# The second layer's modulation as sums along rows on VectorE

## The reference, cut to what matters

```python
mod_l = jnp.split((jax.nn.silu(c) @ w_mod[i] + b_mod[i])[:, None, :], N_MOD, axis=-1)
mod_c = jnp.split((jax.nn.silu(c_ctx) @ w_mod[i] + b_mod[i])[None, None, :], N_MOD, axis=-1)
h_l = modulate(rms_norm(x, norm1_g[i]), mod_l[0], mod_l[1])
...
x = x + mod_l[2] * y_l
x = x + mod_l[5] * squared_relu_mlp(modulate(rms_norm(x, norm2_g[i]), mod_l[3], mod_l[4]), w_mlp1[i], w_mlp2[i])
```

## Time and profile before

| | us |
|---|---|
| median of 3 runs | 3865.7 |
| lowest and highest run | 3863.07, 3866.2 |
| the profiled execution, span from first to last instruction | 3859.4 |
| TensorE busy in it | 3717.8 |
| VectorE busy in it | 1794.7 |
| ScalarE busy in it | 1380.8 |

### The profile page before, as it was taken

One profiled execution on the slowest core, in us unless ns is written; L12 is line 12 of the kernel. 1 busy time (PEld: TensorE's weight loads), 2 busy tenths in 40 slices (PEclk: granted clock), 3 DMA queues, 4 the chain that ended last, 5 costly groups with the idle time before them and its releaser, 6 DMA issues.

```text
span 3859.4 us, 65224 instructions
## 1 busy us (share of the span) xinstructions
PE 3717.8 (96%) x27522; PEld 3332.3 (86%) x27522; DVE 1794.7 (47%) x3201; ACT 1380.8 (36%) x2792; POOL 467.9 (12%) x564
## 2 busy tenths in 40 slices
PE   7999899999999999999999999999998999999998
PEld 7877777888888887888888789999997888999998
DVE  4454555233234556544455564443445556444444
ACT  3544443122123444422422352342233235234232
POOL 1122220000002422100111100110012110011001
PEclk9999999999999999999999999999999999999999
DMA  5211122333331211232311112222221111222222
GB/s 186 71 61 61 51 76 71 110 105 109 106 108 61 66 51 63 79 98 94 118 50 41 49 50 91 85 83 88 89 86 40 45 55 50 91 90 84 93 93 72
DMA packets 88129, 306.09 MB, mean 79 GB/s; under 512 B 10000, under 2 KB 13200, under 8 KB 87712
## 3 DMA queue, kind: packets, MB, share of 16 engines
q1 hardware_dynamic: 85184, 293.25, 22.7%
q0 software_dynamic: 2656, 8.68, 0.7%
HBM read 299.79 MB, written 2.10 MB: 78 GB/s over the span
## 4 chain that ended last, share of the span: by engine, by line
PE 90%; DVE 4%; ACT 3%; POOL 1%; issue 1%; DMA 0%; SPq 0%; POOLq 0%; DVEq 0%; ACTq 0%
PE bank L576 65%; PE bank L638 6%; PE bank L1089 2%; PE bank L607 2%; PE bank L875 2%; PE bank L914 1%; PE bank L1075 1%; PE bank L733 1%; PE bank L820 1%; PE bank L942 1%; PE bank L967 1%; PE bank L1214 1%; PE bank L954 1%; PE bank L1185 1%; DVE weight_lo L1870 1%
## 5 line engine op out<-in xcount | busy, mean ns | idle before, releaser
L1870 DVE TENSOR_TENSOR weight_lo<-weight_raw,weight_hi 128x1024 fp32r<-128x1024 f32 (+1 forms) x464 | 557.7, 1204 | 552.3 <-ACT weight_hi L1283 552.2
L1283 ACT ACTIVATE weight_hi<-weight_raw 128x1024 fp32r<-128x1024 f32 (+1 forms) x464 | 476.9, 1031 | 617.4 <-PE bank L576 371.3
L576 PE MATMUL bank<-u_hi,weight_hi 128*128 128x256 f32 (+1 forms) x2112 | 611.6, 290 | 2.5 <-DVE weight_lo L1870 2.3
L576 PE MATMUL bank<-u_lo,weight_hi 128*128 128x256 f32 (+1 forms) x2112 | 599.2, 284 | 0.0
L576 PE MATMUL bank<-u_hi,weight_lo 128*128 128x256 f32 (+1 forms) x2112 | 598.4, 283 | 0.0
L576 PE MATMUL bank<-h_hi,weight_hi 128*128 128x512 f32 (+1 forms) x1328 | 484.9, 365 | 16.0 <-DVE h_lo L2283 9.2
L576 PE MATMUL bank<-h_lo,weight_hi 128*128 128x512 f32 (+1 forms) x1328 | 465.1, 350 | 0.0
L576 PE MATMUL bank<-h_hi,weight_lo 128*128 128x512 f32 (+1 forms) x1328 | 464.9, 350 | 0.0
L576 PEld LDWEIGHTS bank<-u_hi,weight_hi 128*128 128x128 f32 x2112 | 399.7, 189 | 28.7 <-issue 23.0
L576 PEld LDWEIGHTS bank<-u_hi,weight_lo 128*128 128x128 f32 x2112 | 399.5, 189 | 0.0
L576 PEld LDWEIGHTS bank<-u_lo,weight_hi 128*128 128x128 f32 x2112 | 398.5, 189 | 0.1
(11 more groups left out here) (279 smaller groups left out, 7375.4 us busy)
## 6 DMA issues: line engine op xcount, KB each, us to landing
weight_raw<-in_w_mlp SPq DMA_DIRECT2D x128, 512.0 KB, 3.5
weight_raw<-in_w_ff SPq DMA_DIRECT2D x128, 512.0 KB, 3.5
weight_raw<-in_w_in SPq DMA_DIRECT2D x92, 512.0 KB, 3.4
weight_raw<-in_w_mod SPq DMA_DIRECT2D x80, 512.0 KB, 4.4
weight_raw<-in_a_w_qkv SPq DMA_DIRECT2D x24, 512.0 KB, 3.8
weight_raw<-in_b_w_qkv SPq DMA_DIRECT2D x24, 512.0 KB, 3.5
first_weight<-in_w_mod SPq DMA_DIRECT2D x16, 512.0 KB, 15.3
weight_raw<-in_w_ret_o SPq DMA_DIRECT2D x16, 512.0 KB, 3.5
```

The lines of the kernel that those rows point to most:

```text
L576: m = e.matmul(view[:, 0:hi - lo], a[:, k, :], b[:, k0 + k, lo:hi], start=(k == 0 and i == 0), stop=(k == kt - 1 and i == 2))
L1283: e.activation(whi[s % N_SPLIT][:, 0:kt, :], raw[n % N_RAW][:, 0:kt, :], ACT.Copy).then_inc(*tick("act_split", ("hi", n)))
L1870: e.tensor_tensor(wlo[s][:, 0:kt, :], raw[n % N_RAW][:, 0:kt, :], whi[s][:, 0:kt, :].bitcast(F32), ALU.subtract).then_inc(*tick("dve_split ...
```

## The change

The second layer's modulation leaves TensorE. `w_mod1` is laid out on the host as its transpose: tile m holds 128 features on the partitions and the 1024 rows of the matrix along the free axis, again 512 KB. Both condition vectors are laid out on all 128 partitions (`c_rows`, 1 MB), loaded from POOL's queue behind the fence `wo` of the first layer into `vector_rows`, which takes the place of the axial table and the rotation's scratch, and put through Silu by ScalarE in the first turn of the side work. For each tile VectorE then runs two SCALAR_TENSOR_TENSOR instructions, one for each vector: product of tile and vector element by element, with the sum along the row (`accum_out`) as a column of `MOD`. The product itself is thrown away, the first into rows 4 and 5 of the scratch, the second over the tile. The second instruction releases the raw buffer. One addition of all biases follows the last tile. The tiles are spread over 53 turns in place of 56. ScalarE waits for the last sums before it squares for the second layer's norm, since that uses the same scratch.

```diff
+        CROWS = sb("vector_rows", [P, 2, D], F32, o_lcl)
...
+        PRODUCT = SCR[:, 4:6, :].rearrange("p a b -> p (a b)")[:, 0:D]
...
+            def modulation_loads(layer):
+                for m in range(6 * KT):
+                    done_with[weight((f"w_mod{layer}", m), split=False)] = ("modp", layer, m)
+                    yield
...
-            last = diffusion_layer(0, modulation(0, 2 * KT, 6 * KT, True),
-                                   paced(modulation(1, 0, 6 * KT, False), 6 * KT, 56))
+            last = diffusion_layer(0, modulation(0, 2 * KT, 6 * KT, True), paced(modulation_loads(1), 6 * KT, 53))
...
-                    e.wait_ge(*(at("modq", layer, m0 - 2) if m0 else at("modq", layer - 1, 46)))
+                    e.wait_ge(*at("modq", layer, m0 - 2))
...
+            def vector_rows():
+                e.wait_ge(*at("crows"))
+                e.activation(CROWS[:, :, :], CROWS[:, :, :], ACT.Silu).then_inc(*tick("act_mod", ("crowss",)))
+                yield
...
                     if q == 3 and layer == 0:
+                        e.wait_ge(*at("modp", 1, 6 * KT - 1))
                         square(("n1", 1), m, span, x_all(m, N_ALL), "xm", layer, q, m)
...
+            def modulation_rows(layer):
+                e.wait_ge(*at("crowss"))
+                for m in range(6 * KT):
+                    n = number[f"w_mod{layer}", m]
+                    w = raw[n % N_RAW][:, :, :].rearrange("p k c -> p (k c)")
+                    e.wait_ge(*at("raw", n))
+                    e.wait_ge(*at("modp", layer, m - 1))
+                    for s, to in enumerate((PRODUCT, w)):
+                        e.scalar_tensor_tensor(out=to, in0=w, scalar=1.0, in1=CROWS[:, s, :], op0=ALU.mult, op1=ALU.mult,
+                                               accum_out=mod_row(layer, m, s)).then_inc(
+                            *tick("dve_mod", ("modp", layer, m)))
+                    if m + 1 < 6 * KT:
+                        yield
+                e.wait_ge(*at("modp", layer, 6 * KT - 1))
+                both = MOD[layer][:, :].rearrange("p (m s) -> p m s", s=2)
+                e.tensor_tensor(both, both, vec("b_mod", 48 * layer, 48).unsqueeze(2).to_broadcast([P, 48, 2]),
+                                ALU.add).then_inc(*tick("dve_mod", *(("modd", layer, m) for m in range(6 * KT))))
+                yield
...
-            diffusion_layer(0, modulation(0, 2 * KT, 6 * KT, True),
-                            paced(modulation(1, 0, 6 * KT, False), 6 * KT, 56))
+            diffusion_layer(0, modulation(0, 2 * KT, 6 * KT, True), paced(modulation_rows(1), 6 * KT, 53))
...
                 fence("wo", layer)
+                if layer == 0:
+                    e.dma_start(CROWS[:, :, :].rearrange("p s k -> p (s k)"), t["c_rows"]).then_inc(
+                        *tick("dma_crows", ("crows",), by=16))
...
+    both = np.stack([a["c"].reshape(-1), a["c_ctx"].reshape(-1)])
+    out["c_rows"] = np.ascontiguousarray(np.broadcast_to(both.reshape(1, -1), (P, 2 * D)))
...
-        out[f"w_mod{i}"] = tiles_of(a["w_mod"][i])
+        out[f"w_mod{i}"] = np.ascontiguousarray(a["w_mod"][i].T.reshape(-1, P, D)) if i else tiles_of(a["w_mod"][i])
```

More of the change, by code:

```diff
@@ L496, in mod, with mod_row @@
             return MOD[layer][:, j:j + 1]
+        def mod_row(layer, m, s):
+            return MOD[layer][:, 2 * m + s:2 * m + s + 1]
         def source(key):
@@ L1829, in scalar_program @@
             first_norm()
-            diffusion_layer(0, modulation(0, 2 * KT, 6 * KT, True),
-                            paced(modulation(1, 0, 6 * KT, False), 6 * KT, 56))
+            diffusion_layer(0, modulation(0, 2 * KT, 6 * KT, True), vector_rows())
             m0, w = KT - TURN, "b_w_qkv"
```

## The result

The changed kernel takes 3900.5 us (median of 4 runs, 3896.9 to 3905.2) against 3865.2 before (4 runs): the ratio is 1.0091, 95% interval 1.0078 to 1.0105. It is slower, by 35 us where 58 were forecast.

The account below looks back on a forecast made before the run. TensorE was taken as the bound, busy 96%. Its 53 products going from 488.1 to 543.6 us give +55.5, the Silu +2.5: +58.0, so 3923 us; likeliest case 3903 to 3944, wider range 3894 to 3966.

Parts of the forecast that it names:

- the likeliest case: Whole kernel: the late release makes TensorE wait for weights; 3923 us, own range 3903 to 3944, chance 78%.
- What leaves TensorE: First layer's MLP: 48 modulation tiles at 0.81 us and 24 turnings at 0.30 leave TensorE, 46.1 us in all.
- Where the buffer comes free: Raw-weight ring: the buffer is freed by VectorE's second sum behind `hidden_lo`, 5.4 us later than by TensorE before.
- The term D: Price on VectorE of one new instruction with its sum: 1.35 us, within 1.20 to 1.50.
- the walk: Turn-by-turn count of the ring over 53 MLP turns: 543.6 us against 488.1 before, +55.5.
- The landing: Weight load in the MLP, from going out to ScalarE's start on the high half: 3.66 us.
- The loop: VectorE, SP's queue and ScalarE from load to next load: 11.46 us per w1 turn, 9.76 per w2 turn.
- The Silu: ScalarE's Silu over 128x2048 in turn 3, with table load: the first two sums wait for it, +2.5 us.
- The waits: TensorE idle until `weight_lo` between 620 and 1180 us: some 24 waits of 3 us and 16 of 1.4.
- Half rate: Rival: VectorE's new instruction takes two cycles per element, D 2.4, +147, with Silu about 4015 us; chance 11%.
- The clock: Rival: TensorE's clock falls after waits; every second w1 product at 1.2 GHz costs 62 more, 3985 us; chance 4%.
- The ring: Rival: the raw-weight ring hides the late release, TensorE never waits, full gain of 46, 3820 us; chance 5%.

Follow-up runs that it names:

- the second measurement: The changed kernel itself, unaltered, measured again on chip 7 beside the kernel before: 3910.0 us, ratio 1.0112.
- the sums at the head: Changed kernel with the first layer's MLP side work moved to the head of each turn on VectorE, the Silu likewise on ScalarE: 3818.4 us, ratio 0.9881.

## Why the prediction was right, and where its size was off

The direction and the mechanism were right: TensorE waits for weights whose buffer VectorE releases late. The size was too high by 23 us, and 3900.5 stands below the low end of the likeliest case. It lies inside the wider range only through the 9 us below 3903 that no term of the sum accounts for, which is luck; the second measurement, 3910.0, lies in the likeliest case's own range.

**What leaves TensorE** (46.1 us): right. It shows only where nothing else binds: with the sums at the head the marks come 46.3 us closer, and TensorE is busy 47.0 us less between them.

**Where the buffer comes free**: right. SP's waits end with the second sum in 47 cases, and the line that moves only the release costs 58 us.

**The term D**: this is the step that was mis-sized. I took 1.35 for a sum, within 1.20 to 1.50; it is 1.145, below what I had called the least it could be. The linear step of the earlier trace rows gave 1.29 where the record is 1.22, and I added 0.15 for the read-out, which lies wholly under the next instruction. At 8.6 us for each 0.1 that is 17.6 us, the largest part of the 23 by which the forecast was high; the landing was too high as well, and what the walk lacked took some of both back. The slope itself was confirmed from both sides: 1.15 us more per tile made +47.7, 1.15 less made -38.8 (there some of the turns of the second matrix leave the loop for TensorE's own 8.34).

**The landing**: 3.66, from issue to ScalarE's start, was taken from one pair of rows. In the profile of the changed kernel it was 3.39 on average (3.37 to the landing and 0.02 to the start), in the second one 3.56. By the prediction's own 4.3 us for each 0.1 the first is 11.6 us less than forecast.

**The loop**: with D of 1.145 and a landing of 3.56, as in the two rounds shown, the prediction's terms give 3.56 + 5.00 + 2.29 + 0.10 = 10.95 for the turns of the first matrix; the rows have 10.93. For the second matrix's, with the 3.37 that the load issued at 689.35 took to land, 3.37 + 3.30 + 2.29 + 0.10 = 9.06, and the rows have 9.07. The whole walk with D of 1.145 gives, with the Silu, +29 for a landing of 3.39 and +36 for 3.56, against 35.0 and 42.6 between the marks. Some 6 are left in both. The trace shows three things that the walk didn't have: where two weights load together behind a turn without a tile, the second took 4.0 to 4.4 us to land and the next weight 4.1 to 4.4; there was one wait of 1.3 for `hidden_lo`; and the clock bound two turns, as shown next.

**The Silu**: right. ScalarE in order of time at the first tile:

```profile
632.15 1.28 ACT L1412 ACT_TABLE_LOAD   x1
633.44 1.92 ACT L1412 ACTIVATE vector_rows<-vector_rows 128x2048 f32<-128x2048 f32 x1
```

`hidden_hi` of that turn ends at 632.14, the Silu at 635.36, and the first sum waited 2.3 us for it, against 2.5.

**The waits**: TensorE waited 41 times for a low half, 56.4 us in all, as expected in number. Most are shorter than the 3 and 1.4 us expected, for the loop was shorter: 1.9 to 2.5 in the turns of the first matrix, or 0.3 to 0.8 behind a slowed product and in a quarter's first turns, and mostly 0.2 to 0.9 in those of the second. Three are longer: 5.4 at the first tile, where the Silu comes in, and 3.2 and 3.1 later. Two neighbours show what the clock did:

```profile
768.70 0.47 PE L581 MATMUL bank<-h_hi,weight_hi 128*128 128x512 f32 x1 [2.40 <-DVE weight_lo L1887]
...
779.63 0.47 PE L581 MATMUL bank<-h_hi,weight_hi 128*128 128x512 f32 x1 [0.77 <-DVE weight_lo L1887]
```

Both products start 10.93 us apart, one after 2.40 us idle, the other after 0.77: the product between filled its wait. The windows over its first 5.3 us and the rest show why (columns as in the earlier trace rows):

```profile
768.70:774.00 5.30, 5.30 (x16) 4.23 (x17) 3.96 (x6) 0.84 (x1) 0.00 (x0) 0.68 0.00 0
774.00:779.60 5.60, 4.86 (x33) 4.33 (x32) 1.34 (x2) 1.93 (x3) 0.00 (x0) 1.00 0.53 187
```

After the wait of 2.40 the granted clock was 0.68 over 5.3 us, between its levels of 1.2 and 2.4 GHz, so in part at the lower one, and full after that. The mean granted clock over the window of 400 us is 0.98, against 1.00 before.

From 640 to 1130 us the granted clock fell nine times, for 3.4 us each; before, it never fell in this stretch. Each fall came with or just behind a wait of 1.9 to 5.4 us, and eight other waits of such length had none. A slowed product takes 10.0 us in place of 8.34. Seven times TensorE still had to wait for the next weight, so that the wait took up nearly all of it. Twice it didn't: the products that start at 686.13 and 925.53 are followed by the next without idle time. Both have a mean granted clock of 0.83:

```profile
686.13:696.13 10.00, 10.00 (x49) 8.60 (x50) 5.08 (x8) 1.06 (x1) 0.00 (x0) 0.83 0.30 107
925.53:935.54 10.01, 10.01 (x49) 8.63 (x49) 5.23 (x7) 1.46 (x3) 0.00 (x0) 0.83 0.28 101
```

And both stand in the chain of work that ended last, the second together with the product behind it:

```profile
686.13 10.17 PE bank L581 x48
...
925.53 18.52 PE bank L581 x96
```

Behind the first, VectorE waited 0.61 us for the product before its residual addition at 696.33, ahead of the next sums; behind the second comes a turn without a tile, whose product began 1.7 us late. So these two falls cost some 2.3 us, an estimate from these rows.

**The rivals.** Half rate is refuted: 1.22 us, and 4 ns between the instruction with and without a sum. The Trainium skill, Vector Engine (DVE) Microarchitecture Reference, "Points that are easy to get wrong", states the halving for two inputs wider than bf16; the trace doesn't agree. The second instruction that the Trainium skill, VectorE: DVE Perf Modes, "Two Vector instructions with no wait between them", counts for an accumulator output is there, and the trace agrees with that (its record is 0.08 us); it costs no time of its own. The clock fell nine times, and seven falls went into the wait, as the rival's text had it for short falls; two came through, for some 2.3 us, far from the rival's 62. The ring didn't hide the late release; with buffers of their own for the tiles it does.

## What to carry to other kernels

Before work is moved to an idle engine, look at what the moved instruction releases: in a ring that is shared with the critical stream, the place of the release in the new engine's order is worth more than the work. Write down the loop that goes through it (release, load, split, the engine's other work, release) with each duration, and compare it with the bound engine's turn; here 10.9 and 9.1 in the two kinds of turn against 8.3 decided it, and VectorE at half load said nothing. Then try the same work earlier in the turn before adding buffers: the product it was queued behind was not one that it needed.

## What the runs showed of the hardware

A SCALAR_TENSOR_TENSOR of 128x1024 in 32 bits from SBUF takes 1.22 us with or without a sum along the row; the read-out's record of 0.08 us lies under the next instruction. A VectorE instruction that waits for nothing starts some 0.08 us before the record ahead of it ends, so that a row of them counts 1.14 to 1.15 us each.

The time of a 512 KB load from issue to landing isn't a constant of the kernel. Its median was 3.4 in one profile and 3.7 in another, in the same stage of the same program, and in the first one it went from 3.2 or 3.3 to 3.4 to 3.6 and back. The second of two weights issued 0.42 us apart took 4.0 to 4.4. In a loop that holds the load, 0.17 us of mean landing went with 7.5 us between the marks.

TensorE's granted clock can fall with short waits: here nine of 17 waits of 1.9 to 5.4 us went with a fall of 3.4 us to the lower level, and a product of 8.34 us then takes 10.0.
